# Both products of a squared-ReLU MLP as one level of Strassen, in two phases with the hidden activations in DRAM

## The chip, the core and the metric

The kernel runs on one core of a Trainium2 chip. The metric is the device time of one execution in microseconds (us), taken as the median over the runs. PE is TensorE (matrix products), DVE is VectorE, ACT is ScalarE, POOL is GpSimd and SP is SyncE, which issues most DMAs. Each engine works through its own instructions in order; semaphores order the engines among each other.

## The reference, cut to what matters

The program computes two transformer blocks, one behind the other, on 1024 tokens of width 1024. The part that changes is the MLP of the first block, with the norm behind it and the first norm of the second block. The modulation of the second block does not depend on the tokens, and the kernel computes it beside the MLP.

```python
def sq_relu_mlp(h, up_w, down_w):                  # h 1024x1024, up_w 1024x4096, down_w 4096x1024
    return jnp.square(jax.nn.relu(h @ up_w)) @ down_w

def first_block(...):
    ...
    h = h + sq_relu_mlp(rmsnorm(h, norm_mlp_w), mlp_up_w, mlp_down_w)
    return rmsnorm(h, norm_f_w)

def second_block(x, c, ctx, c_ctx, w_ada, b_ada, ...):
    mod = jax.nn.silu(c) @ w_ada[l] + b_ada[l]             # 1024 x 6144, and the same for c_ctx
    ...
    h = modulate(rmsnorm_2(x, g_mix[l]), sh1, sc1)
    q, k, v, bg, cg, hv = jnp.split(h @ w_in[l], SPLIT_POINTS, axis=-1)
```

## The kernel before

Every product of this kernel is done in three passes: each float32 operand is split into a high part (a copy rounded to fp32r) and a low part (the rest), and `mm3` issues high·high, low·high and high·low into the same PSUM bank (lines L432 to L434). ACT makes the high parts (L419 for weights, L548 for transposed activations), DVE the low parts (L426, L555). A matmul has 128x128 stationary values and 512 moving columns.

The MLP stands in `mlp_block(f)` on PE, ACT and DVE, for eight blocks of 512 hidden features. On PE a block is 192 matmuls of the up product (8 tiles of 128 features by 512 tokens, with 8 slices of the inner dimension and 3 passes each), then 192 of the down product (8 tiles of 128 tokens, 2 halves of 512 columns, 4 slices, 3 passes). Behind each up tile ACT takes the ReLU out of PSUM (L1252), DVE squares it (L1858), ACT makes its high part (L1244) and DVE its low part (L1829): the hidden activations never leave SBUF. Behind each down tile DVE adds the tile to the residual rows `x_tokens` in SBUF (L1872). SP loads the weights of the next half block while this one runs. The blocks 2 to 6 are hardware loops.

Beside the blocks the modulation is summed: POOL loads `ada_w` in 48 pieces of 512 KB, DVE multiplies each with one column per row and adds it to `ada_sums` (L1844 for the first, L1847 for the others, four instructions a piece while both vectors c and c_ctx are summed, then two), and once per block PE sums the partitions in up to four small matmuls (L2590), which ACT copies out (L1263).

Ahead of the MLP the last projection of the attention (`gemm_tokens(B_XO + 1, ...)`) runs over the eight tiles of 128 tokens. Behind each tile come its residual add (L650), the norm (ACT L515 and L518, DVE L526), eight transposes on PE (L541), and high and low parts. Behind the MLP the final norm of block one (ACT L586, DVE L595) and the first norm of block two (L515, L526, and the shift row L530) run row by row beside the last block, and the query projection of block two starts when the first rows are transposed. The projection to keys and values, with 256 columns a matmul, follows it.

Of the kernel before, what the change touches and what calls it, by code (L numbers as in the profile page):

```python
# [29 lines left out]
P = 128  # L30
S = 1024
# [69 lines left out]
def build(nc, x, mem, positions, norm_mix_w, w_in, conv_w, conv_b, conv_ln_w, conv_ln_b, ret_gn_w, w_out,  # L101
# [6 lines left out]
    acc_d = nc.dram_tensor("expert_sums", (S, D), F32, kind="Internal").ap()  # L108

# [189 lines left out]
    with ExitStack() as stack:  # L299
# [41 lines left out]
        T_ML = len(owners)  # L341
        for _ in range(NFB):
            plan(8, "a")
            plan(16, "d")
# [3 lines left out]
        B_I2 = B_ML + 2 * NFB  # L348
        B_W2 = B_I2 + 5
        LAST = {}  # L350
        for b_, n_ in ((B_IN, T_C + 8), (1, T_C + 16), (2, T_QK + 8), (3, T_V + 8), (4, T_G + 8), (B_WO, T_WO + 8),
                       (B_WO + 1, T_WO + 16), (B_KV, T_MK + 4), (B_KV + 1, T_MK + 8), (B_KV + 2, T_MV + 2),
                       (B_KV + 3, T_MV + 4), (B_XQ, T_XQ + 8), (B_XR, T_XR + 8), (B_XO, T_XO + 8),
                       (B_XO + 1, T_XO + 16), (B_ML, T_ML + 8), (B_ML + 1, T_ML + 24), (B_I2 - 1, T_ML + 24 * NFB),
                       (B_I2, T_Q2 + 8), (B_I2 + 1, T_CG + 4), (B_I2 + 2, T_HV + 4), (B_I2 + 3, T_BG + 4),
                       (B_I2 + 4, T_BG + 8), (B_W2, T_W2 + 8), (B_W2 + 1, T_W2 + 16)):
            LAST[b_] = n_ - 1
# [72 lines left out]
        def mm3(o_, lh, ll, rh, rl, start, stop):  # L430
# [3 lines left out]
            return nc.tensor.matmul(o_, ll, rh, start=False, stop=stop)  # L434

# [232 lines left out]
        ada_n, ada_free, ada_acc = sem("ada_products"), sem("ada_piece_used"), sem("ada_acc")  # L668
# [21 lines left out]
        u_sq, u_hi, u_lo = sem("hidden_squared"), sem("hidden_hi_made"), sem("hidden_lo_made")  # L690
# [41 lines left out]
        def _(sp):  # L732
# [20 lines left out]
            def up_piece(f, half):  # L753
                return mlp_up_w[:, bass.ds(f * FB, FB)].rearrange("(k p) n -> p k n", p=P)[:, 4 * half:4 * half + 4, :]

            def down_piece(f, half):
                return mlp_down_w[bass.ds(f * FB + 2 * P * half, 2 * P), :].rearrange("(k p) n -> p k n", p=P)

            def two_rows(half):
                return raw[:, half, :, :].rearrange("p (k a) n -> p k (a n)", a=2)  # L760

            for half in range(2):
                sp_load(B_ML, half, mlp_up_w[:, 0:FB].rearrange("(k p) n -> p k n", p=P)[:, 4 * half:4 * half + 4, :])
            with sp.Fori(0, NFB - 1) as f:
                for half in range(2):
                    sp.wait_ge(w_ready, f * 8 + 4 * B_ML + 2 * (half + 1))
                    sp.dma_start(two_rows(half), down_piece(f, half)).then_inc(w_raw[half], 16)
                for half in range(2):
                    sp.wait_ge(w_ready, f * 8 + 4 * (B_ML + 1) + 2 * (half + 1))
                    sp.dma_start(raw[:, half, :, :], up_piece(f + 1, half)).then_inc(w_raw[half], 16)  # L770
            for half in range(2):
                sp.wait_ge(w_ready, 4 * (B_I2 - 2) + 2 * (half + 1))
                sp.dma_start(two_rows(half), mlp_down_w[(NFB - 1) * FB + 2 * P * half:(NFB - 1) * FB + 2 * P * (half + 1), :]
                             .rearrange("(k p) n -> p k n", p=P)).then_inc(w_raw[half], 16)
            for b in range(B_I2, B_W2 + 2):
                for half in range(2):
                    src, w = w_source(b, half)
                    sp_load(b, half, src, w)
# [46 lines left out]
        def _(pool):  # L825
# [86 lines left out]
            row(GAIN[:, :], norm_mlp_w, gain_in)  # L912
            pool.wait_ge(nm_tp, 2 * N_B2)
            pool.wait_ge(bias_in, 32)

            def mod_store(f, i):

                pool.wait_ge(mod_made, 2 * (f - 1) + (i + 1))
                pool.sem_inc(pool_link, 1)
                pool.dma_start(mod_d[:, bass.ds(1024 * (f - 1) + 512 * i, 512)], MODB[64 * i:64 * i + 2, i, :],  # L920
                               accum_op=ALU.add).then_inc(mod_out[i], 16)

            def ada_loads(f, first=False):

                for i in range(8):
                    if not first:
                        pool.wait_ge(ada_free, 8 * (f - 1) + (i - 1))
                    elif i >= 2:
                        pool.wait_ge(ada_free, i - 1)
                    k = 2 * (i % 4)  # L930
                    pool.dma_start(ADR[:, i % 2, :, :], w_ada_2[0, P * k:P * (k + 2), bass.ds(1024 * (f - 1) + 512 * (i // 4), 512)]
                                   .rearrange("(k p) n -> p k n", p=P)).then_inc(ada_in[i % 2], 16)
                    if i == 1 and not first:
                        mod_store(f - 1, 1)
                mod_store(f, 0)

            ada_loads(1, first=True)
            with pool.Fori(2, NFB - 1) as f:
                ada_loads(f)
            mod_store(NFB - 2, 1)  # L940
            for n in range(2):
                pool.wait_ge(mod_out[n], 16 * (ADA_COLS // 2))
            row(GAIN[:, :], g_mix_2[0], mod_in)
            row(XN[:, 0, :], mod_d[0, D:2 * D], mod_in)
            row(SHIFT[:, :], mod_d[0, 0:D], mod_in)
            row(GF[:, :], norm_f_w, mod_in)

            pool.wait_ge(acc_ready, T_ML + 24 * NFB)
            pool.dma_start(CX[:, 0, :], ctx_2[0, tok(0), :]).then_inc(rows_in, 16)
            pool.dma_start(CX[:, 1, :], ctx_2[0, tok(1), :]).then_inc(rows_in, 16)  # L950
            row(GC[:, :], g_mix_2[0], rows_in)
            row(CSC[:, :], mod_d[1, D:2 * D], rows_in)
            row(SHC[:, :], mod_d[1, 0:D], rows_in)
            for t in range(NT):
                pool.wait_ge(pl_x, t + 1)
                pool.dma_start(xsave_d[tok(t), :], X[:, t, :]).then_inc(x_saved, 16)
            pool.wait_ge(x_saved, 16 * NT)
# [76 lines left out]
        def _(act):  # L1034
# [204 lines left out]
            residual_act(B_XO, T_XO, N_MLP)  # L1239

            def hidden_hi(m, f):
                h, c = m // 4, m % 4
                act.wait_ge(u_sq, f * 8 + m + 1)
                act.activation(UH[:, c, h * 512:(h + 1) * 512], UF[:, m % 2, :], ACT.Copy).then_inc(u_hi, 1)  # L1244

            def mlp_block(f):
                for m in range(8):
                    if m == 7:
                        split_hi(B_ML + 1, off=2 * f)
                    act.wait_ge(acc_ready, f * 24 + T_ML + m + 1)  # L1250
                    act.wait_ge(u_lo, f * 8 + m + 1)
                    act.activation(UF[:, m % 2, :], acc(T_ML + m), ACT.Relu).then_inc(acc_act, 1)  # L1252
                    if m >= 1:
                        hidden_hi(m - 1, f)
                hidden_hi(7, f)

            def mod_copy(f, i, first=False):

                act.wait_ge(ada_acc, 2 * (f - 1) + 2)
                if not first:  # L1260
                    act.wait_ge(mod_out[i], 16 * (f - 1))
                rows = slice(64 * i, 64 * i + 2)
# [1724 lines left out]
```

## Time and profile before

| | |
|---|---|
| median of 3 runs | 2503.62 us (2503.07 to 2506.1) |
| span of the profiled execution, first to last instruction | 2512.2 us |
| PE busy in the span | 97% |
| DVE, ACT, POOL busy in the span | 65%, 42%, 9% |
| TensorE clock granted over the span | 0.985 of full |

All stretches and durations below come from the one profiled execution, whose span is 2512.2 us, 0.34% over the median. Only its span is known, no time around it. A window is given as two times from the start of the span; the MLP of the first block runs from about 697 to 1408 us in it.

### The profile page before, as it was taken

The numbers are of one execution on the slowest core, as the hardware profiler recorded it, in microseconds if no ns is written. First come the engines' busy times: TensorE is split into PE (matmuls) and PEld (weight loads), VectorE is DVE, ScalarE is ACT, GpSimd is POOL, SyncE is SP. The second block draws the span as 40 slices with busy tenths as digits, with TensorE's granted clock in tenths as the row PEclk, the third lists the DMA queues.
The fourth block names the chain that finished last, engine by engine and source line by source line (L and its number), as shares of the span: only waits on it lengthen the run. The fifth ranks groups of instructions, "written<-read, shape, count | busy, mean of one in ns | idle before, by whom it ended". The sixth has DMA issues, their size and how long they took to land.

```text
span 2512.2 us, 31048 instructions
## 1 busy us (share of the span) xinstructions
PE 2442.1 (97%) x12148; PEld 2003.7 (80%) x12148; DVE 1621.1 (65%) x2049; ACT 1056.6 (42%) x1549; POOL 224.7 (9%) x232
## 2 busy tenths in 40 slices
PE   9999899999999999999999999999999999999996
PEld 7788788888888888888888798866786888888884
DVE  7999834324444564444444862477467999999987
ACT  5234523433331222212123422176254777777765
POOL 1000600000000000001010100000113121111101
PEclk9999899999999999999999999999998999999998
DMA  4110221401121232323231311010228999999988
GB/s 154 67 43 34 81 86 43 151 18 42 34 84 57 90 105 84 101 83 117 84 99 69 143 35 51 34 35 18 86 110 306 365 381 398 393 395 394 394 330 304
DMA packets 116317, 370.27 MB, mean 147 GB/s; under 512 B 6309, under 2 KB 15701, under 8 KB 116208
## 3 DMA queue, kind: packets, MB, share of 16 engines
q1 hardware_dynamic: 94832, 293.63, 30.9%
q0 software_dynamic: 21376, 75.12, 9.5%
q8 instruction: 77, 1.26, 0.2%
q14 instruction: 32, 0.26, 0.0%
HBM read 343.50 MB, written 25.26 MB: 147 GB/s over the span
## 4 chain that ended last, share of the span: by engine, by line
PE 86%; DVE 9%; ACT 2%; DMA 2%; issue 1%; SPq 0%; POOLq 0%; DVEq 0%; ACTq 0%
PE banks L432 24%; PE banks L434 24%; PE banks L433 24%; DVE conv_out L1618 3%; PE banks L2769 1%; PE banks L541 1%; PE banks L2567 1%; PE banks L2534 1%; PE banks L2736 1%; DVE w_lo L426 1%; DVE expert_w_lo L2187 1%; PE banks L2702 1%; PE banks L2703 1%; DMA expert_w<-in_w_up 1%; PE banks L2429 1%
## 5 line engine op out<-in xcount | busy, mean ns | idle before, releaser
L2187 DVE TENSOR_TENSOR expert_w_lo<-expert_w,expert_w_hi 128x2048 fp32r<-128x2048 f32 x189 | 426.8, 2285 | 27.3 <-ACT expert_w_hi L1452 26.0
L1452 ACT ACTIVATE expert_w_hi<-expert_w 128x2048 fp32r<-128x2048 f32 x192 | 366.9, 1918 | 151.6 <-PE banks L434 127.3
L432 PE MATMUL banks<-act_hi,w_hi 128*128 128x512 f32 x960 | 375.2, 391 | 0.2 <-DVE act_lo L555 0.2
L434 PE MATMUL banks<-act_hi,w_lo 128*128 128x512 f32 x960 | 373.7, 389 | 0.0
L433 PE MATMUL banks<-act_lo,w_hi 128*128 128x512 f32 x960 | 373.5, 389 | 0.0
L419 ACT ACTIVATE w_hi<-w_raw 128x1024 fp32r<-128x1024 f32 x152 | 159.3, 1060 | 262.7 <-PE banks L434 262.7
L432 PE MATMUL banks<-w_hi,act_hi 128*128 128x512 f32 (+1 forms) x640 | 247.8, 387 | 12.7 <-DVE w_lo L426 10.4
L426 DVE TENSOR_TENSOR w_lo<-w_raw,w_hi 128x1024 fp32r<-128x1024 f32 x152 | 188.3, 1251 | 106.5 <-ACT w_hi L419 100.3
L434 PE MATMUL banks<-w_hi,act_lo 128*128 128x512 f32 (+1 forms) x640 | 244.3, 382 | 0.0
L433 PE MATMUL banks<-w_lo,act_hi 128*128 128x512 f32 (+1 forms) x640 | 244.0, 381 | 0.0
L434 PEld LDWEIGHTS banks<-act_hi,w_lo 128*128 128x128 f32 x960 | 180.2, 188 | 37.7
L432 PEld LDWEIGHTS banks<-act_hi,w_hi 128*128 128x128 f32 x960 | 180.2, 188 | 37.4 <-DVE act_lo L555 0.5
L433 PEld LDWEIGHTS banks<-act_lo,w_hi 128*128 128x128 f32 x960 | 180.2, 188 | 37.0
L432 PE MATMUL banks<-expert_w_hi,expert_rows_T_hi 128*128 128x512 f32 x512 | 201.4, 393 | 3.8 <-DVE expert_w_lo L2187 3.3
L432 PE MATMUL banks<-w_hi,hidden_hi 128*128 128x512 f32 x512 | 200.2, 391 | 0.0
L434 PE MATMUL banks<-expert_w_hi,expert_rows_T_lo 128*128 128x512 f32 x512 | 199.5, 390 | 0.0
L434 PE MATMUL banks<-w_hi,hidden_lo 128*128 128x512 f32 x512 | 199.3, 389 | 0.0
L433 PE MATMUL banks<-w_lo,hidden_hi 128*128 128x512 f32 x512 | 199.3, 389 | 0.0
L433 PE MATMUL banks<-expert_w_lo,expert_rows_T_hi 128*128 128x512 f32 x512 | 199.2, 389 | 0.0
L1872 DVE TENSOR_TENSOR x_tokens<-x_tokens,banks 128x512 f32<-128x512 f32 x128 | 86.9, 685 | 146.6 <-PE banks L434 145.3
L1858 DVE TENSOR_TENSOR hidden_f<-hidden_f 128x512 f32<-128x512 f32 x64 | 44.3, 692 | 180.5 <-ACT hidden_f L1252 180.5
L432 PEld LDWEIGHTS banks<-w_hi,act_hi 128*128 128x128 f32 x640 | 121.6, 190 | 37.4 <-DVE w_lo L426 8.8
(442 smaller groups left out, 4147.7 us busy)
## 6 DMA issues: line engine op xcount, KB each, us to landing
expert_w<-in_w_gate SPq DMA_DIRECT2D x32, 2048.0 KB, 11.5
expert_w<-in_w_up SPq DMA_DIRECT2D x32, 2048.0 KB, 11.6
expert_w<-in_w_down SPq DMA_DIRECT2D x32, 2048.0 KB, 11.1
ada_w<-in_w_ada POOLq DMA_DIRECT2D x48, 512.0 KB, 4.2
w_raw<-in_mlp_up_w SPq DMA_DIRECT2D x16, 1024.0 KB, 5.4
w_raw<-in_mlp_down_w SPq DMA_DIRECT2D x16, 1024.0 KB, 4.9
w_raw<-in_w_in SPq DMA_DIRECT2D x10, 1024.0 KB, 5.3
w_raw<-in_w_in SPq DMA_DIRECT2D x18, 512.0 KB, 6.1
```

The lines of the kernel that those rows point to most:

```text
L419: nc.scalar.activation(WH[:, 2 * j:2 * j + 2, 0:width], raw[:, half, 2 * (j % 2):2 * (j % 2) + 2, 0:width], ACT.Copy).then_inc(w_hi, 1)
L426: nc.vector.tensor_tensor(WL[:, 2 * j:2 * j + 2, 0:width], raw[:, j // 2, 2 * (j % 2):2 * (j % 2) + 2, 0:width], WH[:, 2 * j:2 * j + 2, 0: ...
L432: nc.tensor.matmul(o_, lh, rh, start=start, stop=False)
L433: nc.tensor.matmul(o_, lh, rl, start=False, stop=False)
L434: return nc.tensor.matmul(o_, ll, rh, start=False, stop=stop)
L541: m = nc.tensor.transpose(BK[4 + q % banks][:, c * P:(c + 1) * P], (XN[:, i % 2, :] if src is None else src)[:, k * P:(k + 1) * P], IDN)
L1452: act.activation(EWH[ring][:, 2 * j:2 * j + 2, :], EW[slot][:, 2 * j:2 * j + 2, :], ACT.Copy).then_inc(w_hi, 1)
L1618: dve.scalar_tensor_tensor(out=dst, in0=src, scalar=VT[:, c, j:j + 1], in1=dst, op0=ALU.mult, op1=ALU.add).then_inc(conv_n, 1)
L1858: dve.tensor_tensor(UF[:, m % 2, :], UF[:, m % 2, :], UF[:, m % 2, :], ALU.mult).then_inc(u_sq, 1)
L1872: dve.tensor_tensor(xs, xs, acc(n), ALU.add).then_inc(acc_dve, 1)
L2187: dve.tensor_tensor(EWL[slot][:, c, :], EW[slot][:, c, :], EWH[ring][:, c, :], ALU.subtract).then_inc(w_ready, 1)
L2429: m = pe.matmul(y_bank(t)[:, DV * h:DV * (h + 1)], ST[:, t % 2, h, :], V[:, t, DV * h:DV * (h + 1)], start=(t == 0 and h == 0), stop=(h == ...
```

## The change

The MLP is taken out of `mlp_block` and written as two phases, all unrolled.

**Up phase.** Per block of 512 hidden features the product of weights (1024 x 512) and tokens (1024 x 1024) is cut into 2 by 2 quarters and formed from seven products in place of eight (Winograd's form of Strassen), each 256 features x 512 tokens x 512 inner, that is 24 matmuls. The list `UP` orders the 56 products; below, item n is the n-th of them. The sums of token quarters are formed once, beside the last tiles of the attention projection (`act_sums`, `act_parts`, and on POOL `act_lo_pool`); the sums of weight quarters are formed per block by DVE (`up_sums`), three items ahead of PE. Results are added up partly in PSUM, partly by ACT copies from bank to bank (`copy_p1`) and DVE adds (`c22`, `c12`). The squared hidden values go to DRAM (`hid_d`), and the residual rows are parked there too (`xpark_d`).

**Down phase.** Four chunks of the inner dimension, each of seven Strassen products `M1` to `M7`, each product in two items of 24 matmuls: 56 items. DVE forms the sums of hidden and of weight quarters and the low parts (`down_parts`), ACT the high parts (`down_hi`). ACT also writes a product's running sum back into PSUM ahead of it (`seed`) and reads it out behind it (`evict`).

**Behind them.** POOL combines the seven sums in five adds of 128 x 2048 (`f_z`), DVE in six of 128 x 1024 (`x11`, `x21`, `x22`). Only then do the norms start. For token tiles 3 to 7 POOL adds the shift row of the second norm. PE transposes the first row tile ahead of the last down item.

**The modulation.** DVE's pieces stand behind the items listed in `ADA_PIECES`, and PE's small matmuls (`mou_sums`) ahead of the item behind that (`MOD_AT`).

```diff
@@ the two lists @@
+        UP = [("P1", 0), ("P2", 0), ("P1", 1), ("P5", 0), ("P6", 0), ("P7", 0), ("P4", 0), ("P3", 0)]
+        for b_ in range(1, NFB):
+            UP += [("P5", b_), ("P6", b_), ("P2", b_), ("P7", b_)] + ([("P1", b_ + 1)] if b_ + 1 < NFB else []) + [("P4", b_), ("P3", b_)]
...
+        DOWN = [("M3", ("A11",), ("B12", "B22", ALU.subtract)), ("M5", ("A11", "A12", ALU.add), ("B22",)),
+                ("M4", ("A22",), ("B21", "B11", ALU.subtract)), ("M1", ("A11", "A22", ALU.add), ("B11", "B22", ALU.add)),
+                ("M7", ("A12", "A22", ALU.subtract), ("B21", "B22", ALU.add)), ("M2", ("A21", "A22", ALU.add), ("B11",)),
+                ("M6", ("A21", "A11", ALU.subtract), ("B11", "B12", ALU.add))]
...
+            n_ = (0 if UP[k_][0] == "P1" else 1) if q_ < 16 else (2 if UP[k_][0] in ("P6", "P2") else 1)
+            ADA_PIECES[k_] = range(q_, min(q_ + n_, 48))
...
+        MOD_AT = {k_ + 1: q // 4 for k_, qs in ADA_PIECES.items() for q in qs if q % 4 == 3}
@@ PE @@
-            mlp_block(0, first=True)
...
-            mlp_block(NFB - 1, after=lambda t: norm_transpose(N_B2 + t - 3) if t >= 3 else None)
+            for n in range(NU):
+                kind, b = UP[n]
+                pe.wait_ge(u_lo, n + 1)
+                if n in MOD_AT:
+                    mou_sums(MOD_AT[n])
...
+                        if n == 0 and j == 0 and k == 3:
+                            up_banks_read(6)
+                            begin_banks()
...
+                    if n == 0 and j == 0:
+                        up_transpose(7)
...
+            for n in range(ND - 1):
+                down_sub(n)
+            pe.wait_ge(d_ev, d_ev0 + 2 * (NP - 2))
+            pe.wait_ge(xf, xf0 + 6)
+            norm_transpose(N_B2)
+            down_sub(ND - 1)
+            norm_transpose(N_B2 + 1)
@@ DVE, up phase @@
+            for k in range(NU):
...
+                if done == "P7":
+                    c22(db, 1)
+                if done == "P3":
+                    c12(db, 1)
+                if k + 3 < NU:
+                    up_sums(k + 3)
+                    up_lo(k + 3)
...
+                if kind == "P3":
+                    c12(b, 0)
+                for q in ADA_PIECES.get(k, ()):
+                    ada_piece(q)
@@ ACT, down phase @@
+            for k in range(ND - 4):
+                g = k // 2
+                if k % 2 == 0 and g >= 1:
+                    evict(g - 1, 1)
+                down_hi(k + 3)
+                if k % 2 == 0 and g + 1 in SEED_NO:
+                    seed(g + 1)
+                if k % 2 == 1 and g < NP - 3:
+                    evict(g, 0)
@@ POOL @@
+            for t in range(4, NT):
+                act_lo_pool(t)
...
+            pool.tensor_tensor(DACC["M6"], DACC["M1"], DACC["M3"], ALU.add).then_inc(f_z, 1)
+            pool.wait_ge(f_z, f_z0 + 4)
+            pool.wait_ge(d_ev, d_ev0 + 2 * m7 + 2)
+            pool.tensor_tensor(DACC["M6"], DACC["M6"], DACC["M2"], ALU.subtract).then_inc(f_z, 1)
```

Three places show how the instructions stand.

DVE in the up phase, around items 5 to 8, after the change (`up_w_lo` are low parts of weight operands three items ahead, `hidden_stage_dve` the adds and squares of finished hidden tiles, `ada_sums` the modulation):

```order
L2358 SCALAR_TENSOR_TENSOR ada_sums<-ada_w,silu_c,ada_sums 128x512 x4
L2273 TENSOR_TENSOR up_w_lo<-up_w_123,up_w_hi 128x1024
L2380 TENSOR_TENSOR hidden_stage_dve<-up_sum_u_136,banks 128x512
L2364 SCALAR_TENSOR_TENSOR hidden_stage_dve<-hidden_stage_dve 128x512
L2358 SCALAR_TENSOR_TENSOR ada_sums<-ada_w,silu_c,ada_sums 128x512 x4
L2380 TENSOR_TENSOR hidden_stage_dve<-up_sum_u_136,banks 128x512
L2364 SCALAR_TENSOR_TENSOR hidden_stage_dve<-hidden_stage_dve 128x512
L2294 TENSOR_TENSOR up_w_sums<-up_w_odd,up_w_121 128x1024
L2273 TENSOR_TENSOR up_w_lo<-up_w_sums,up_w_hi 128x1024
```

The second `ada_sums` row is the last of the first four pieces: it stands last in DVE's step beside item 7, and PE's small matmuls ahead of item 8 wait for it. Before the change the pieces stood between adds to the residual:

```order
L1872 TENSOR_TENSOR x_tokens<-x_tokens,banks 128x512 x2
L1847 SCALAR_TENSOR_TENSOR ada_sums<-ada_w,silu_c,ada_sums 128x512 x4
L1872 TENSOR_TENSOR x_tokens<-x_tokens,banks 128x512 x2
L1847 SCALAR_TENSOR_TENSOR ada_sums<-ada_w,silu_c,ada_sums 128x512 x4
L1872 TENSOR_TENSOR x_tokens<-x_tokens,banks 128x512 x6
```

There the small matmuls came behind the sixth of the eight token tiles, and a piece was only followed by residual adds and low parts of later weights.

ACT in the down phase, one product of two items after the change (L1614 high parts, L1624 reads a product out of PSUM, L1645 writes the running sum of a later one into PSUM):

```order
L1624 ACTIVATE x_tokens<-banks 128x2x512 x2
L1614 ACTIVATE down_a_hi<-down_a_sums 128x1024
L1614 ACTIVATE t_hi<-t_plain 128x1024
L1645 ACTIVATE banks<-x_tokens 128x1024 x2
L1614 ACTIVATE down_a_hi<-down_a_sums 128x1024
L1614 ACTIVATE act_hi<-act_hi_plain 128x2x512
L1624 ACTIVATE act_lo_plain<-banks 128x2x512 x2
```

None of these stood there before: the residual was added by DVE (L1872).

DVE at the end of the down phase, after the change (the first row is the low part of the last item's operand; L634 and L565 are the rows of the two norms, L2443 are adds of `x21`):

```order
L2405 TENSOR_TENSOR t_lo<-t_plain,t_hi 128x1024
L2483 SCALAR_TENSOR_TENSOR second_gain_row<-x_normed,second_gain_row 128x1024
L633 RECIPROCAL rms_scale<-root_mean_square 128x1
L634 SCALAR_TENSOR_TENSOR x_tokens<-x_tokens,rms_scale,gain_row_final 128x1024
L633 RECIPROCAL rms_scale<-root_mean_square 128x1
L634 SCALAR_TENSOR_TENSOR x_tokens<-x_tokens,rms_scale,gain_row_final 128x1024
L563 RECIPROCAL rms_scale<-root_mean_square 128x1
L565 SCALAR_TENSOR_TENSOR x_normed<-x_tokens,rms_scale,second_gain_row 128x1024
L569 TENSOR_TENSOR x_normed<-x_normed,second_shift_row 128x1024
L633 RECIPROCAL rms_scale<-root_mean_square 128x1
L634 SCALAR_TENSOR_TENSOR x_tokens<-x_tokens,rms_scale,gain_row_final 128x1024
L2443 TENSOR_TENSOR x_tokens<-x_tokens,banks 128x2x512
```

Behind these come the row tile 1 (L563, L565, L569) and the second L2443. The first transposes of PE wait until that second L2443 is done, and the last down item stands behind the transposes. Before, the norms ran row by row beside the last block's matmuls.

## Rows read from the trace of the kernel before

**Rows 1.** The page, part 1: busy time, share of the span, instructions

```profile
PE 2442.1 (97%) x12148; PEld 2003.7 (80%) x12148; DVE 1621.1 (65%) x2049; ACT 1056.6 (42%) x1549; POOL 224.7 (9%) x232
```

**Rows 2.** Windows: busy time by engine, granted clock, DMA share, GB/s

```profile
697.00:1408.00 711.00, 711.00 (x3155) 582.12 (x3154) 358.02 (x488) 170.97 (x258) 47.58 (x64) 1.00 0.26 86
```

**Rows 3.** The chain that ended last, in order of time: start us, us

```profile
1129.38 0.96 PE banks L2590 x4
...
1217.60 0.96 PE banks L2590 x4
```

**Rows 4.** Timeline of PE behind the MLP; brackets: idle before, releaser

```profile
1413.15 0.39 PE L434 MATMUL banks<-w_hi,act_lo 128*128 128x512 f32 x1
1419.80 0.80 PE L432 MATMUL banks<-w_hi,act_hi 128*128 128x512 f32 x1 [6.26 <-DVE w_lo L426]
...
1468.13 0.39 PE L432 MATMUL banks<-w_hi,act_hi 128*128 128x256 f32 x1 [0.26 <-DVE w_lo L426]
```

**Rows 5.** Windows behind that wait, and behind the later one of rows 6

```profile
1420.00:1424.00 4.00, 4.00 (x11) 3.17 (x12) 3.71 (x4) 0.00 (x0) 0.53 (x1) 0.59 1.03 408
...
1638.00:1642.00 4.00, 3.94 (x23) 3.48 (x21) 3.35 (x8) 4.00 (x12) 0.00 (x0) 0.57 0.01 2
```

**Rows 6.** Timeline of PE in the second block's attention

```profile
1637.28 0.38 PE L2702 MATMUL banks<-w_k_hi_T,act_hi 128*128 128x256 f32 x1 [3.29 <-ACT w_probs L1359]
```

**Rows 7.** Groups of DVE instructions by line and form: busy us, mean ns

```profile
L426 DVE TENSOR_TENSOR w_lo<-w_raw,w_hi 128x1024 fp32r<-128x1024 f32 x152 | 188.3, 1251 | 106.5 <-ACT w_hi L419 100.3
L1872 DVE TENSOR_TENSOR x_tokens<-x_tokens,banks 128x512 f32<-128x512 f32 x128 | 86.9, 685 | 146.6 <-PE banks L434 145.3 <-DVE ada_sums L1847 1.2
L526 DVE SCALAR_TENSOR_TENSOR x_normed<-x_tokens,rms_scale,gain_row 128x1024 f32<-128x1024 f32 x39 | 50.1, 1285 | 1.4
```

**Rows 8.** Timeline of DVE: instructions back to back, in single rows of several

```profile
695.82 4.62 DVE L426 TENSOR_TENSOR w_lo<-w_raw,w_hi 128x1024 fp32r<-128x1024 f32 x4
...
835.16 1.37 DVE L1872 TENSOR_TENSOR x_tokens<-x_tokens,banks 128x512 f32<-128x512 f32 x2 [0.45 <-PE banks L434]
...
894.20 2.73 DVE L1847 SCALAR_TENSOR_TENSOR ada_sums<-ada_w,silu_c,ada_sums 128x512 f32<-128x512 f32 x4
```

**Rows 9.** Timeline of ACT at the end of the MLP

```profile
1406.40 3.89 ACT L419 ACTIVATE w_hi<-w_raw 128x1024 fp32r<-128x1024 f32 x4
...
1413.40 1.06 ACT L586 ACTIVATE squares_row<-x_tokens 128x1024 f32<-128x1024 f32 x1 [2.15 <-DVE x_tokens L1872]
1414.36 0.19 ACT L586 ACTIVATION_READ_ACCUMULATOR squares_row<-x_tokens 128x1 f32 x1
1414.58 0.29 ACT L588 ACTIVATE root_mean_square<-sum_squares,eps_col 128x1 f32<-128x1 f32 x1
```

**Rows 10.** Groups of ACT instructions that read PSUM

```profile
L1252 ACT ACTIVATE hidden_f<-banks 128x512 f32<-128x512 f32 x64 | 38.2, 596 | 242.1 <-PE banks L434 241.9 <-DVEq L1894 0.2
...
L1462 ACT ACTIVATE expert_silu<-banks 128x1024 f32<-128x1024 f32 x16 | 16.1, 1006 | 2.2 <-PE banks L434 2.2
```

**Rows 11.** Timeline of POOL beside the conv and the retention

```profile
274.52 2.52 POOL L863 TENSOR_TENSOR conv_out<-conv_out,conv_ln_rstd 128x512 f32<-128x512 f32 x2
276.97 0.75 POOL L883 TENSOR_TENSOR ret_q_decayed<-ret_qk_T,ret_consts 128x256 f32<-128x256 f32 x1
277.66 1.28 POOL L872 TENSOR_TENSOR ret_gate<-ret_gate,ret_gn_row 128x512 f32<-128x512 f32 x1
...
282.29 3.47 POOL L863 TENSOR_TENSOR conv_out<-conv_out,conv_ln_rstd 128x512 f32<-128x512 f32 x2
```

**Rows 12.** Timeline of DVE in the same stretch

```profile
275.15 4.87 DVE L426 TENSOR_TENSOR w_lo<-w_raw,w_hi 128x1024 fp32r<-128x1024 f32 x1
...
283.12 1.51 DVE L426 TENSOR_TENSOR w_lo<-w_raw,w_hi 128x1024 fp32r<-128x1024 f32 x1
```

**Rows 13.** Groups of POOL: the largest elementwise instruction of the kernel before

```profile
L998 POOL TENSOR_TENSOR expert_w_lo<-expert_w,expert_w_hi 128x2048 fp32r<-128x2048 f32 x3 | 13.5, 4548 | 0.0
```

**Rows 14.** The page, DMA issues: KB each, median us to landing

```profile
w_raw<-in_mlp_up_w SPq DMA_DIRECT2D x16, 1024.0 KB, 5.4
```

More of the change, by code:

```diff
@@ new lines, in build, with sub_done @@
+        NCH = 4
+        NP = 7 * NCH
+        ND = 2 * NP
+        SUM_NO, SEED_NO = {}, {}
+        for n_ in range(ND):
+            for side_ in (1, 2):
+                if len(DOWN[n_ // 2 % 7][side_]) == 3:
+                    SUM_NO[n_, side_] = 4 * NFB + len(SUM_NO) + 1
+        for g_ in range(NP):
+            if g_ >= 7 or g_ not in (0, 3, 5):
+                SEED_NO[g_] = 2 * len(SEED_NO)
+        def sub_done(n):
+            return 2 * NU + 3 * (n // 2) + (1 if n % 2 == 0 else 3)
@@ L764, in _, with up_w @@
[L764 to L774, printed above, removed]
+            def up_w(b, kh, fh):
+                c = 512 * b + 256 * fh
+                return mlp_up_w[512 * kh:512 * (kh + 1), c:c + 256].rearrange("(k p) n -> p k n", p=P)
@@ L923, in ada_loads @@
[L923 to L940, printed above, removed]
+                pool.dma_start(mod_d[:, 512 * cb:512 * (cb + 1)], MODB[64 * (cb % 2):64 * (cb % 2) + 2, cb % 2, :],
+                               accum_op=ALU.add).then_inc(mod_out[cb % 2], 16)
+            for q in range(4 * ADA_COLS):
+                if q >= 2:
+                    pool.wait_ge(ada_n, ada_ops(q - 1))
+                kk = 2 * (q % 4)
+                pool.dma_start(ADR[:, q % 2, :, :], w_ada_2[0, P * kk:P * (kk + 2), 512 * (q // 4):512 * (q // 4 + 1)]
+                               .rearrange("(k p) n -> p k n", p=P)).then_inc(ada_in[q % 2], 16)
+                if q >= 4 and q % 4 == 2:
+                    mod_store(q // 4 - 1)
@@ new lines, in second_lo @@
+            def second_lo(t):
+                norm_lo(N_B2 + t, a_hi(t), a_lo(t))
+            dve.wait_ge(mod_in, 64)
+            dve.scalar_tensor_tensor(out=GAIN2[:, :], in0=XN[:, 0, :], scalar=1.0, in1=GAIN2[:, :], op0=ALU.add,
+                                     op1=ALU.mult).then_inc(gain_made, 1)
+            dve.wait_ge(gain_made, 1)
+            first_rows(0)
+            first_rows(1)
+            second_rows(0)
+            first_rows(2)
+            x21(0)
+            second_rows(1)
```

948 lines of the change are left out of this document (739 added, 209 removed).

## The prediction

> **What bounds the kernel now.** I began with the page: PE is busy 97% of the span, DVE 65%, ACT and POOL far less [rows 1]. A share over the span says nothing of one stage, so next came the window of the MLP. In its 711 us PE is busy for all 711 at a granted clock of 1.00, DVE for 358, ACT for 171, POOL for 48 [rows 2]: the stage is bound by the number of matmuls and by nothing else. The chain in time order gives their price. The modulation matmuls of two successive blocks begin 88.22 us apart, and they take 0.96 [rows 3], so 384 matmuls last 87.26 us, 0.2272 each, and 24 of them, an item of the new program, 5.45.
>
> Behind the MLP the timeline of PE shows the one real stall: 6.26 us for the low part of a query weight that stands behind the norm rows in DVE's queue, later another 0.26 [rows 4]. The window behind the first shows what such idleness costs beyond itself: clock 0.59 of full, and 11 matmuls in 4 us where 17.6 fit [rows 5], 1.5 us lost. A wait of 3.29 us elsewhere [rows 6] is followed by 0.57 as well [rows 5]. Stalls of some 3 us therefore have a tail; 0.26 had none in view.
>
> **What is removed.** The products go from 8 x 384 matmuls to 112 items of 24, that is 3072 to 2688: 384 fewer, **−87.3 us**. Two matmuls that open PSUM banks add **+0.5**. The 12 modulation sums stay. The end of the MLP is rewritten, so its old stalls go: 6.26 + 1.5 + 0.26 = **−8.0**. All else must be paid out of these 94.8 us, and is paid by DVE, ACT and POOL.
>
> **Start of the up phase.** Unit prices first. A 128x1024 DVE instruction with two SBUF inputs takes 1.16 back to back (4.62 for four), a 128x512 one 0.69, a modulation piece of four 2.73 [rows 8]. On ACT a 128x1024 copy takes 0.97 (3.89 for four) [rows 9], a 128x512 one out of PSUM 0.60 [rows 10]. For each of the token tiles 4 to 7 DVE now has six differences (4.1), the residual add (0.7) and the norm row (1.3, [rows 7]), 6.1 us in the time of a tile, 5.45 plus its transposes. So it has no reserve, and ahead of the last tile three low parts (3.5) are put in as well. PE then waits for the norm of tile 6, for the differences of tile 6 ahead of the bank openers in item 0, and for the norm of tile 7 behind half of item 0. I estimate 1.4, 1.4, 4.0 and 2.0 plus 1.2 at the lower clock, **+10**; bounds 0 (all in reserve of the three items of lead) and 16 (the whole 3.5 + 6.1 + 6.1). POOL's twelve small differences there, 1.28 each by [rows 11], can hold DVE up: +2, bounds 0 and 4. Taken **+12**.
>
> **Up phase.** A block of seven items takes PE 38.1 us. DVE's work for one: three sums, one further sum and seven low parts (11 x 1.16 = 12.8), eight instructions on finished hidden tiles (5.5), six or seven modulation pieces (16.4 to 19.1): 34.7 to 37.4. That fits barely, and each sum must go to ACT and come back before its low part. The operands have three items of lead, which covers this. The modulation has none: the fourth piece of a column block stands last in DVE's step beside item k, and PE's sums stand ahead of item k+1. Beside item 7, ACT first reads a tile, copies two banks, squares two (5 x 0.60) and makes the high part (0.97); DVE's low part (1.16), add and square (1.4) and the piece (2.73) follow: 9.2 us from the item's start against 5.45, a wait of 3.8. Item 22 repeats it; items 12 and 17 give about 2.8. The eight later sums have pieces of half the length, and I put them at 1 each with the waits of P5 for the adds of the block before: 13.2 + 8 = 21. Two of the waits are as long as the 3.29 with a tail of 1.5 each: **+24**. Bounds 0 (if ACT's share is done ahead of time) and 35 (every step late by as much as the worst, 2.8 for all twelve).
>
> **Down phase.** Per item DVE has three or four instructions of 1.16, at most 4.6 of 5.45; ACT per product four high parts, two seeds and two reads of 128x1024: 4 x 0.97 + 4 x 1.0 (PSUM reads 1.006 [rows 10]; a write into PSUM of this size has no row, between 0.97 and twice that) = 7.9 of 10.9. Loads on SP's queue are 512 KB, a 1024 KB one lands in 5.4 us [rows 14], against a lead of 16. So **0**. What hides ACT is its 3.0 us of slack per product; gone, each further microsecond costs 28.
>
> **End.** The norms used to run row by row beside the last block's matmuls. Now nothing can start before the seven sums are combined. The transposes ahead of the last item wait for the second x21 add. Behind its last operand DVE has a gain row (1.2), three final-norm rows and two second-norm rows (five of 1.29, and two shifts of 1.16), and two adds of 1.16: 12.3, with the reciprocals between them about 13, and some 3.3 of ACT statistics (1.06 + 0.19 + 0.29 each [rows 9]) that nothing covers. DVE's own step beside item 52 (four instructions and an add, 5.9) stands ahead, so the chain ends 22.2 us after item 52's start; PE is through items 52 to 54 after 16.3: a wait of 5.9, plus a tail of 1.5. The context rows now come last and hold up their transposes by 1 to 3, and the first weight for keys and values waits for them (5): **+14**, bounds 8 and 20. POOL's five adds of 128x2048, 4.55 each [rows 13], fall into the same stretch. [rows 12] show what that can do: a low part of 1.25 mean [rows 7] took 4.87 while POOL ran three instruction groups back to back at their normal pace, and another took 1.51 while POOL's pair took 3.47 instead of 2.52 [rows 11]. So either may lose. On the chain DVE can lose 17 (two POOL adds and most of two more) or 0; I take **+9**, the middle, since the two rows disagree on the loser. Five shift rows on POOL, 2.3 each as half of 4.55, mostly beside the query matmuls: **+2.5**, bounds 0 and 12.
>
> The Trainium skill, "SBUF — State Buffer", section "Who interferes with whom", says that a DVE instruction with two SBUF inputs contends with a GpSimd instruction that reads SBUF, and under an exclusive lock. The 4.87 agrees with a lock, the 1.51 only partly; by the rule alone the nine would be up to seventeen.
>
> **Sum:** −87.3 + 0.5 − 8.0 + 12 + 24 + 14 + 9 + 2.5 = −33.3 us, so the profiled execution of 2512.2 would become 2479. That span is 8.6 us above the median of the runs shown; the same difference taken from 2503.6 gives **2470 us**.
>
> **The rivals.**
>
> *B, the vector engines keep pace* (0.18). If ACT's copies run ahead and POOL yields, the up phase costs 8, the start 10, the end 14: gain 94.8 − 32 = 63, about 2441. For it: DVE's total fits into 38.1 per block. Against: its order in the queue, which no average changes.
>
> *C, the port and the queues cost their upper part* (0.20). DVE blocked for 17 at the end, 6 for shift rows, start 16, up phase 30, end 14: 83, gain 12, about 2491; at still higher prices within 5 us of no change. For it: [rows 12]. Against: POOL lost in one of the two.
>
> *D, ACT's queue becomes the bound of the down phase: slower* (0.09). ACT's high part waits for a DVE sum, and the seed of the next product stands behind it. With 3.0 us of slack and 28 products, the gain of 33 is gone when a product takes ACT 3.0 + 1.2 = 4.2 us more than its 7.9, and at 5 more the time is 2470 + 28 x 2 = 2526. For it: the sums start only when the buffer of an item earlier is free, so four trips from DVE to ACT and back fall into each product. Against: each trip has three items to do so.
>
> That the change does not do what it says is excluded here: the program holds 2688 of these matmuls.
>
> **How the numbers follow.** The forecast has 0.50, with its own range of 2456 to 2484; B 0.18, around 2441; C 0.20, of which 0.04 within 5 us of 2503.6; D 0.09; the remaining 0.03 near no change. Faster and slower count from 0.2%, or 5 us, about what this kernel's measurement can tell from no change: faster 0.50 + 0.18 + 0.16 = 0.84, same 0.07, slower 0.09. The range of 2436 to 2497 leaves out a little of B, D and the part of C near no change, 0.2 together.
>
> **What would show it.** PE busy should fall by some 87 us in the stretch from 690 to 1470, and waits of PE should appear: of `mou_sums` for `ada_sums`, 2 to 4 us each at items 8, 12, 17 and 22; of the bank openers for act_lo; of the first transposes for `x_normed` at the end, 6 to 15 us; and none in the down phase. DVE rows of 128x1024 well over 1.3 us beside POOL's 128x2048 adds show the port; if they stay at 1.2 while POOL's exceed 4.6, POOL yields and the 9 goes. Waits of the down items for `seed` or high parts would show D. The prediction is wrong if the up phase stalls in most items, if the clock stays low beyond the tails, or if PE waits for its own instructions now that no loop repeats them, for which I have no row.

## The result, and the profile after

The changed kernel takes 2516.56 us (median of 8), the kernel before 2504.07 beside it. The ratio is 1.005 with a 95% interval of 1.0032 to 1.0067: slower by half a per cent, some 12.5 us, where 2470 had been forecast. The profiled execution has a span of 2528.0 us, 15.8 more than that of before; it is the slowest of its eight. Up to the first transposes of the MLP's norm the two traces are level (659.54 us before, 659.72 after). At the first scores of the second block's attention the changed kernel is 12.5 us behind (1625.1 and 1637.6); the other 3.3 lie behind that, where the program is the same.

The page of the changed kernel, part 1:

```profile
PE 2396.9 (95%) x11766; PEld 1948.2 (77%) x11766; DVE 1798.4 (71%) x2092; ACT 1259.3 (50%) x1759; POOL 282.9 (11%) x254
```

Against [rows 1], PE has 382 instructions fewer and is busy 45 us less: the matmuls did go, but those that are left take longer. PE's idle time, span less busy time, rose from 70 to 131 us, so 45 saved and 61 lost make the 16 of the span. The waits of PE in the stretch from the last attention projection to the first keys and values (us in total, times, longest):

```profile
PE banks L3213 <- issue: 25.3, 9, 4.2
PE banks L580 <- DVE x_tokens L2443: 15.5, 1, 15.5
PE banks L471 <- ACT banks L1645: 5.2, 2, 4.7
PE banks L3195 <- DVE x_normed L565: 4.4, 3, 1.5
PE banks L580 <- DVE ctx_rows L569: 3.5, 1, 3.5
PE banks L465 <- DVE w_lo L459: 3.0, 1, 3.0
PE banks L3245 <- ACT t_hi L1530: 2.4, 1, 2.4
```

L3213 are the modulation matmuls, L580 the transposes (first the row tile 0 of block two, then the context rows), L1645 is a `seed`, L3245 the bank openers. "issue" means that the view names no releaser; the timelines name it. PE and then DVE around item 8:

```profile
760.88 0.39 PE L473 MATMUL banks<-act_hi,up_w_lo 128*128 128x512 f32 x1
764.97 3.42 PE L3213 MATMUL banks<-ada_sums,consts_sb 128*2 128x512 f32 x4 [3.69 <-issue]
768.32 0.50 PE L471 MATMUL banks<-act_hi,up_w_hi 128*128 128x512 f32 x1
```

```profile
759.67 1.22 DVE L2273 TENSOR_TENSOR up_w_lo<-up_w,up_w_hi 128x1024 fp32r<-128x1024 f32 x1 [2.43 <-ACT up_w_hi L1510]
760.81 0.68 DVE L2380 TENSOR_TENSOR hidden_stage_dve<-up_sum_u,banks 128x512 f32<-128x512 f32 x1
761.52 0.69 DVE L2364 SCALAR_TENSOR_TENSOR hidden_stage_dve<-hidden_stage_dve 128x512 f32<-128x512 f32 x1
762.13 2.73 DVE L2358 SCALAR_TENSOR_TENSOR ada_sums<-ada_w,silu_c,ada_sums 128x512 f32<-128x512 f32 x4
```

DVE's piece ends at 764.86 and PE goes on at 764.97: this is the wait that was forecast, of the size that was forecast (3.8). What was not forecast stands in the same row: the modulation matmuls themselves, four rows of the trace (each such matmul is recorded as two), take 3.4 us, where four took 0.96 before [rows 3]. The groups of these matmuls before and after, busy us and mean ns, then idle time ahead of them:

```profile
L2590 PE MATMUL banks<-ada_sums,consts_sb 128*2 128x512 f32 x32 | 7.9, 592 | 0.0
```

```profile
L3213 PE MATMUL banks<-ada_sums,consts_sb 128*2 128x512 f32 x32 | 23.0, 837 | 25.3 <-issue 25.3
```

The window over the stretch with all modulation sums, granted clock behind the engines' busy times:

```profile
764.00:1030.00 266.00, 241.45 (x954) 178.63 (x955) 174.32 (x217) 90.07 (x129) 40.90 (x54) 0.94 0.56 172
```

In [rows 2] that clock was 1.00. At the end of the down phase DVE's and POOL's timelines read:

```profile
1351.13 1.23 DVE L2397 TENSOR_TENSOR down_a_sums<-act_lo_plain,w_raw 128x1024 f32<-128x1024 f32 x1 [0.66 <-PE banks L473]
1353.54 4.38 DVE L2405 TENSOR_TENSOR down_a_lo<-down_a_sums,down_a_hi 128x1024 fp32r<-128x1024 f32 x1 [1.19 <-ACT down_a_hi L1614]
1357.84 5.63 DVE L2405 TENSOR_TENSOR act_lo<-act_hi_plain,act_hi 128x1024 fp32r<-128x1024 f32 x1
1363.39 5.61 DVE L2397 TENSOR_TENSOR down_a_sums<-act_lo_plain,w_raw 128x1024 f32<-128x1024 f32 x1
...
1386.48 4.40 DVE L634 SCALAR_TENSOR_TENSOR x_tokens<-x_tokens,rms_scale,gain_row_final 128x1024 f32<-128x1024 f32 x1
...
1399.16 5.40 DVE L569 TENSOR_TENSOR x_normed<-x_normed,second_shift_row 128x1024 f32<-128x1024 f32 x1
```

```profile
1351.15 5.68 POOL L1180 TENSOR_TENSOR x_tokens<-x_tokens 128x2048 f32<-128x2048 f32 x1 [0.29 <-ACT banks L1645]
1356.91 5.48 POOL L1182 TENSOR_TENSOR x_tokens<-x_tokens,act_hi_plain 128x2048 f32<-128x2048 f32 x1
1362.35 5.57 POOL L1184 TENSOR_TENSOR x_tokens<-x_tokens,act_lo_plain 128x2048 f32<-128x2048 f32 x1
1384.86 4.93 POOL L1186 TENSOR_TENSOR x_tokens<-act_lo_plain,act_hi_plain 128x2048 f32<-128x2048 f32 x1 [16.94 <-ACT banks L1645]
1398.49 4.99 POOL L1189 TENSOR_TENSOR x_tokens<-x_tokens,x_top_right 128x2048 f32<-128x2048 f32 x1 [8.70 <-ACT x_top_right L1624]
```

Lay the two side by side: each of the five long DVE rows ends 1.1 us behind the end of one POOL row, about the time that the DVE instruction takes alone. Once a POOL add has begun, a DVE instruction with two SBUF inputs gets through nothing until it ends. The order of the starts matters: the DVE row of 1351.13 began 0.02 us ahead of POOL's first add and took its normal 1.23. Five rows lose about 19 us to it (4.38 + 5.63 + 5.61 + 4.40 + 5.40, less five of 1.2 to 1.3).

### The profile page after: what moved, and what is told of

It reads as the page before. It is cut to its first block, busy times and chain, and to the rows that moved or that the text cites. A ratio compares the mean times of both kernels' runs of the same rounds, so it can differ in the third digit from the quotient of the medians.

```text
span 2528.0 us, 30286 instructions
## 1 busy us (share of the span) xinstructions
PE 2396.9 (95%) x11766; PEld 1948.2 (77%) x11766; DVE 1798.4 (71%) x2092; ACT 1259.3 (50%) x1759; POOL 282.9 (11%) x254
## 4 chain that ended last, share of the span: by engine, by line
PE 76%; DVE 14%; issue 4%; ACT 3%; DMA 1%; POOL 0%; POOLq 0%; SPq 0%; ACTq 0%; DVEq 0%
PE banks L465 15%; PE banks L467 15%; PE banks L466 15%; PE banks L471 6%; PE banks L472 6%; PE banks L473 6%; DVE conv_out L2064 3%; PE banks L3430 1%; PE banks L3179 1%; PE banks L3146 1%; DVE w_lo L459 1%; PE banks L3397 1%; DVE expert_w_lo L2799 1%; PE banks L3213 1%; PE banks L580 1%
## 5 line engine op out<-in xcount | busy, mean ns | idle before, releaser
L465 PE MATMUL banks<-w_hi,act_hi 128*128 128x512 f32 (+1 forms) x640 | 249.3, 389 | 10.5 <-DVE w_lo L459 7.0
L465 PE MATMUL banks<-expert_w_hi,expert_rows_T_hi 128*128 128x512 f32 x512 | 202.2, 395 | 4.0 <-DVE expert_w_lo L2799 3.6
L465 PE MATMUL banks<-act_hi,w_hi 128*128 128x512 f32 x448 | 175.9, 393 | 0.2 <-DVE act_lo L594 0.2
L467 PE MATMUL banks<-act_hi,w_lo 128*128 128x512 f32 x448 | 174.6, 390 | 0.0
L466 PE MATMUL banks<-act_lo,w_hi 128*128 128x512 f32 x448 | 174.5, 389 | 0.0
L2064 DVE SCALAR_TENSOR_TENSOR conv_out<-conv_in,vectors_T,conv_out 128x1024 f32<-128x1024 f32 (+1 forms) x138 | 148.7, 1142 | 3.4 <-ACT conv_out L1312 2.9
L465 PEld LDWEIGHTS banks<-w_hi,act_hi 128*128 128x128 f32 x640 | 122.5, 191 | 35.4 <-issue 7.1
L467 PEld LDWEIGHTS banks<-w_hi,act_lo 128*128 128x128 f32 x640 | 122.3, 191 | 23.5
L466 PEld LDWEIGHTS banks<-w_lo,act_hi 128*128 128x128 f32 x640 | 122.6, 192 | 22.3 <-issue 0.2
L465 PEld LDWEIGHTS banks<-expert_w_hi,expert_rows_T_hi 128*128 128x128 f32 x512 | 96.4, 188 | 24.6 <-DVE expert_w_lo L2799 4.5
L467 PEld LDWEIGHTS banks<-expert_w_hi,expert_rows_T_lo 128*128 128x128 f32 x512 | 96.6, 189 | 20.4
L466 PEld LDWEIGHTS banks<-expert_w_lo,expert_rows_T_hi 128*128 128x128 f32 x512 | 96.7, 189 | 19.4
L471 PE MATMUL banks<-act_hi,up_w_hi 128*128 128x512 f32 x256 | 104.9, 410 | 5.3 <-DVE hidden_stage_dve L2380 2.3
L472 PE MATMUL banks<-act_lo,up_w_hi 128*128 128x512 f32 x256 | 102.6, 401 | 0.0
## 6 DMA issues: line engine op xcount, KB each, us to landing
expert_w<-in_w_up SPq DMA_DIRECT2D x32, 2048.0 KB, 11.4
```

Of the source, the lines that this page charges most:

```text
L465: nc.tensor.matmul(o_, lh, rh, start=start, stop=False)
L466: nc.tensor.matmul(o_, lh, rl, start=False, stop=False)
L471: nc.tensor.matmul(o_, lh, rh, start=start, stop=False, skip_group_check=True)
L472: nc.tensor.matmul(o_, lh, rl, start=False, stop=False, skip_group_check=True)
L2064: dve.scalar_tensor_tensor(out=dst, in0=src, scalar=VT[:, c, j:j + 1], in1=dst, op0=ALU.mult, op1=ALU.add).then_inc(conv_n, 1)
```

## The experiments

All times are ratios to the kernel before, run on the same chip; the changed kernel has 1.005. A difference of 0.001 is 2.5 us. The intervals reach 0.0015 to 0.0031 to either side, so a difference between two kernels below is known to some 6 or 7 us, with e1 to 9. Gains of a few us are read from the traces, and the times only fail to contradict them.

**e1: the modulation matmuls one item later.** DVE's pieces stay where they are.

```diff
-        MOD_AT = {k_ + 1: q // 4 for k_, qs in ADA_PIECES.items() for q in qs if q % 4 == 3}
+        MOD_AT = {k_ + 2: q // 4 for k_, qs in ADA_PIECES.items() for q in qs if q % 4 == 3}
```

> PE's modulation matmuls stand one item later, nothing else moves. Theory (the pieces have no lead, the operands have three items of it): the nine waits before them (25.3 us in the changed kernel) go, with the lower clock that follows each; the matmuls themselves fall from 23.0 us to about 15, at 0.95 a pair. Time falls by 33 to 42, to 2475 to 2484. Rival (DVE is the bound of the up phase, the waits only stand where they stand): the waits reappear in front of matmuls that want up_w_lo or hidden_stage_dve, and the time stays within 10 of 2516.

Ratio 0.9912 (0.9881 to 0.9943): 35 us less than the changed kernel, and faster than the kernel before. The group of the modulation matmuls, and a window over about the same stretch of the program as above (its end lies some 8 us further on):

```profile
L3213 PE MATMUL banks<-ada_sums,consts_sb 128*2 128x512 f32 x32 | 15.7, 591 | 2.3 <-issue 2.3
```

```profile
750.00:990.00 240.00, 233.94 (x981) 178.30 (x981) 176.45 (x221) 89.34 (x128) 41.02 (x54) 1.00 0.63 193
```

The profiled execution of e1 was already 12.9 us ahead at the first transposes of the MLP's norm (646.82), where the program is unchanged, so the spans can't be compared. The same two matmuls in each kernel can, one ahead of the first modulation sum and one behind the last, first in the changed kernel, then in e1:

```profile
755.67 0.39 PE L471 MATMUL banks<-act_hi,up_w_hi 128*128 128x512 f32 x1
...
1078.20 0.39 PE L471 MATMUL banks<-act_hi,up_w_hi 128*128 128x512 f32 x1
```

```profile
741.10 0.39 PE L471 MATMUL banks<-act_hi,up_w_hi 128*128 128x512 f32 x1
...
1029.64 0.39 PE L471 MATMUL banks<-act_hi,up_w_hi 128*128 128x512 f32 x1
```

322.5 us became 288.5: the 34.0 us of this stretch are the gain. In it the waits for the sums fall by 23.0 and the modulation matmuls by 7.3; some 6 come from the matmuls behind, with the clock back at 1.00. The waits do not come back elsewhere: those for `hidden_stage_dve` rise only from 3.1 to 5.3 us in all, which takes 2 off again. DVE was not the bound of the up phase. One item of lead was missing.

**e11: the output rows of the modulation matmuls, in the kernel before.** There the two column blocks of a pair wrote rows 0 and 64 of two banks.

```diff
-                        m = pe.matmul(BK[6 + i][64 * i:64 * i + 2, :], ...
+                        m = pe.matmul(BK[6 + i][0:2, :], ...
```

> The kernel before, with one thing changed: the modulation matmuls of the second column block write output rows 0 and 1, as the first does, and no longer rows 64 and 65; ACT and POOL read them there. Theory (two of these matmuls run side by side when their output rows are 64 apart, and one after the other when not): the group of 32 rows rises from 7.9 us busy to about 15.5, four of them from 0.96 to 1.8; time slower by 5 to 9, 2509 to 2513. Rival (they were quick because they alternated between two banks, which they still do): 7.9 us stays, and the time too.

Ratio 1.0021 (1.0001 to 1.004). The group, and four of them in the chain in time order:

```profile
L2590 PE MATMUL banks<-ada_sums,consts_sb 128*2 128x512 f32 x32 | 14.7, 592 | 0.0
```

```profile
1131.23 1.81 PE banks L2590 x4
```

The time is 5 us (0 to 10) over the kernel before, as forecast. 0.96 became 1.81, although the two banks still alternate. So the pairs had run side by side because their output rows lay 64 apart; the change, which sums one column block at a time, put them one behind the other. Each single row lasts 592 ns in the kernel before and in e11, and 591 in e1: a mean per instruction does not show it, the busy time of the group does.

**e2: POOL's five adds left out.** The output lacks these sums.

```diff
-            pool.tensor_tensor(DACC["M7"], DACC["M4"], DACC["M5"], ALU.subtract).then_inc(f_z, 1)
...
+            pool.sem_inc(f_z, 3)
...
+            pool.sem_inc(f_z, 2)
```

> POOL's five adds of 128x2048 are left out, so the output lacks these sums; everything that waited for them still waits for what they waited for. Theory (POOL's adds hold DVE up through the shared port): DVE's rows of 4.4 to 5.6 us go back to 1.2, PE's wait of 4.75 for a seed goes, the wait of 15.5 ahead of the first transposes falls to about 8; time falls by 12 to 17, to 2500 to 2505. Rival (the chain of norms alone sets that wait, the long rows only look long because DVE waits for something else): under 4 us, and the long rows stay.

Ratio 0.9973 (0.9956 to 0.999): 19 us less, where 12 to 17 had been expected. DVE's row that had taken 5.63, and the last shift row:

```profile
1348.22 1.22 DVE L2400 TENSOR_TENSOR act_lo<-act_hi_plain,act_hi 128x1024 fp32r<-128x1024 f32 x1
...
1374.47 1.23 DVE L569 TENSOR_TENSOR x_normed<-x_normed,second_shift_row 128x1024 f32<-128x1024 f32 x1
```

The seed's wait of 4.7 is gone, and the wait ahead of the transposes is 5.1 in place of 15.5, less than the 8 expected here and close to the 5.9 that the prediction had for the chain without POOL.

**e3: the five adds on DVE.**

```diff
+                if k == ND - 7:
+                    f_z1()
+                if k == ND - 6:
+                    f_z2()
+                if k == ND - 5:
+                    f_z3()
```

(`f_z1` to `f_z5` hold POOL's instructions and waits; the last two stand behind the second x21 and ahead of the first x22.)

> The same five adds on DVE in place of POOL: three in its steps beside items 49 to 51, two behind the second x21 add. Theory (port): DVE works 11.6 us more and loses none of the 20 that it lost to POOL; the seed's wait goes or shrinks under 2, the wait ahead of the transposes is 8 to 12; time falls by 4 to 10, to 2506 to 2512. Rival (DVE's queue is the chain at the end, more work on it costs as much): no change within 3, or slower.

Ratio 1.0021 (1.0006 to 1.0036): 7 us less than the changed kernel. DVE does each add in 2.28 us, 11.4 in all, and no row beside them is long; the wait ahead of the transposes is 9.6. Time, adds and wait came as expected. The adds are cheaper there than the 19 us that they cost on POOL.

**e4: all shift rows on DVE.**

```diff
-        SHIFT_POOL = 3
+        SHIFT_POOL = NT
```

> All eight shift rows of the second norm on DVE; in the changed kernel tiles 3 to 7 had them on POOL. Theory (port): DVE works 5 x 1.2 us more and gets back some 2.2 on each of five rows that took 3.45 beside POOL, so the waits of 3.5 for the context rows and 3.0 for the first low part of the key weights shrink by 3 to 5 together; time falls by 2 to 6, to 2511 to 2515. Rival (DVE is what everything waits for there, so its own five rows cost the 6 us that POOL had hidden): slower by 2 to 6.

Ratio 1.0019 (1.0004 to 1.0034): 8 us less, where 2 to 6 had been expected; the difference is within the noise. In the changed kernel four rows of the final norm (the expectation says five) started with one of POOL's shift rows and took 3.45:

```profile
1427.02 3.45 DVE L634 SCALAR_TENSOR_TENSOR x_tokens<-x_tokens,rms_scale,gain_row_final 128x1024 f32<-128x1024 f32 x1
```

```profile
1426.99 2.38 POOL L1202 TENSOR_TENSOR x_normed<-x_normed,second_shift_row 128x1024 f32<-128x1024 f32 x1 [2.17 <-DVE x_normed L2476]
```

3.45 is 2.38 and 1.28 less a little. With e4 each takes 1.28, the wait for the context rows falls from 3.5 to 1.5, and one of 1.2 for `act_lo` goes. DVE rows with one input in PSUM were not held up: `rotary_tmp_first<-banks,consts_sb` took its usual 0.41 at 1452.83 and 1453.49, beside POOL's fifth shift row.

**e5: two of three weight operands split behind the last token tile's work.**

```diff
-                        for n in range(3):
-                            up_lo(n)
+                        up_lo(0)
...
+            up_lo(1)
+            up_lo(2)
```

(and the high parts on ACT likewise)

> At the start of the up phase only the first of three weight operands is split ahead of the last token tile's work, the other two behind it, on ACT and on DVE. Theory (three low parts stand in the way of the differences that the bank openers want): the waits of 2.41 ahead of the openers and 1.31 ahead of the last transposes go, with some of the lower clock behind them; time falls by 3 to 6, to 2511 to 2514. Rival (the same waits only move to the matmuls of the next two items): no change within 2.

Ratio 1.0047 (1.0031 to 1.0063): no change. The openers wait 1.6 in place of 2.4, but the third item then waits longer for its bank:

```profile
715.48 0.47 PE L471 MATMUL banks<-act_hi,up_w_hi 128*128 128x512 f32 x1 [3.23 <-ACT hidden_stage_act L1573]
```

In the changed kernel it was 1.89 there. All the start's waits together are 11.0, against 9.8. The rival holds by the trace (the time alone could still hide a gain of 3 to 6): with this order the waits only stand elsewhere.

**e7: the last down item ahead of the first transposes.**

```diff
-            for n in range(ND - 1):
+            for n in range(ND):
                 down_sub(n)
...
             norm_transpose(N_B2)
-            down_sub(ND - 1)
```

> PE does the last down item ahead of the first transposes of the second block, all else as in the changed kernel. Theory (the order on PE leaves a ready item of 5.4 us standing behind a wait for DVE): the wait of 15.5 ahead of the transposes shrinks by 5.4 to about 10, and the two adds of x22 can start earlier; time falls by 5 to 9, to 2508 to 2512. Rival (DVE's later rows set the start of the queries anyway): the wait moves behind the transposes, no change within 3.

Ratio 1.004 (1.0022 to 1.0058), not told apart from the changed kernel, where 5 to 9 us had been expected. The first wait shrinks to 10.2, and a new one stands behind it, of the first query matmul; the view names no releaser, and DVE's first add of x22 ended 0.1 us ahead of it. Together they are 15.3, as long as the one wait before:

```profile
1397.30 3.58 PE L580 MATMUL banks<-consts_sb,x_normed 128*128 128x128 f32 x16 [10.25 <-DVE x_tokens L2443]
1405.94 0.77 PE L465 MATMUL banks<-w_hi,act_hi 128*128 128x512 f32 x1 [5.06 <-issue]
```

**e6, e8, e9, e10: together.** e6 is e1 with e3; e8 adds e4 and e7; e9 is e1, e3 and e4; e10 is e9 with both x21 adds, and ACT's reads of that product, ahead of the second norm's rows.

> The modulation matmuls one item later and POOL's five adds on DVE, both together. Theory (two separate places, 300 us apart): the gains add up, 34 + 5 = 39, so 2475 to 2480. Rival (what is won in the up phase is lost again in front of the norms, since those wait for DVE and ACT): not under 2483.

> Four edits together: modulation matmuls one item later, the five adds and all shift rows on DVE, the last down item ahead of the transposes. Theory: 34 + 5 + 4 + 6 = 49, so 2464 to 2471, faster than the kernel before by 33 to 40. Rival (the end is one chain on DVE, and only one of the three edits there can count): 2474 to 2478.

> Modulation matmuls one item later, the five adds and all shift rows on DVE; the last down item stays behind the first transposes, as in the changed kernel. Theory now (the end is one chain on DVE, and moving the last item on PE only moved the wait): the same as the four edits together within 3, 2472 to 2478. Rival (the last item's place does count once the port is free): slower than the four edits by 4 to 6, 2479 to 2481.

> The same three edits, and at the end DVE does both x21 adds and ACT both reads of that product ahead of the second norm's rows, so PE's first transposes wait for less. If the wait ahead of the transposes (9.6 with the adds on DVE) is the price: it falls to about 5, and the time by 4 to 5 against the three edits. If DVE's whole chain to the later rows is the price: the wait moves behind to the query matmuls and the time stays within 2.5.

| | ratio | interval | median us |
|---|---|---|---|
| e6 | 0.9884 | 0.9864 to 0.9903 | 2478.97 |
| e8 | 0.9874 | 0.9854 to 0.9894 | 2475.09 |
| e9 | 0.9869 | 0.9846 to 0.9892 | 2472.42 |
| e10 | 0.9864 | 0.9842 to 0.9886 | 2475.72 |

e6 is the sum of its two parts (35 and 7). e8, e9 and e10 are one time within their intervals, and e6 overlaps with them. e8 had been expected at 2464 to 2471 us and e10 4 to 5 us under e9; neither came, and the rivals named there did. PE's two waits at the end, first in e9, then e8, then e10:

```profile
PE banks L580 <- DVE x_tokens L2431: 9.6, 1, 9.6
PE banks L465 <- issue: 4.0, 1, 4.0
```

```profile
PE banks L465 <- DVE x_tokens L2438: 9.7, 1, 9.7
PE banks L580 <- issue: 4.1, 1, 4.1
```

```profile
PE banks L465 <- issue: 8.4, 1, 8.4
PE banks L580 <- DVE x_normed L569: 5.2, 1, 5.2
```

L580 are the transposes, L465 the first query matmul, L2431 the adds of x21 and L2438 those of x22. The two waits sum to 13.6, 13.8 and 13.6: a single chain that ends with DVE's adds of x22 fits all three, and neither PE's order nor the place of x21 moves its end. e9, three small edits, is faster than the kernel before by 1.3% (1.1 to 1.5), some 33 us.

## Why the prediction was wrong

**The gain was there.** PE ran 382 matmuls fewer, and the stages without waits held their pace: behind 1030 us the matmuls ran 0.23 us apart, with waits of 0.5 and less until the 53rd item of the down phase. "Down phase: 0" was right up to that item, and D, ACT's queue as the bound, did not come: the wait of 4.7 for a `seed` at the 53rd is 0.5 in e2, so it belongs to POOL's adds.

**The step that failed first is "The 12 modulation sums stay".** Their count stayed, their price did not: 7.9 us busy in the kernel before (the group of L2590, 32 rows), 23.0 after. Half of the rise is the lost overlap (e11: 14.7; e1: 15.7 at full clock), half the lower clock in which a wait leaves PE. I had priced the waits at 21 with those of P5; they were 25.3, and 3.1 for `hidden_stage_dve`. I had taken two tails of 1.5; behind seven of the nine waits the sums ran slower than at full clock (1.4 to 1.9 us for two rows against 1.02 in e1, 3.2 to 3.4 for four against 1.88), and the clock was 0.94 over 266 us. e1 shows waits, slow sums and tails together as 35 us (34.0 in the trace) that one item of lead takes away. Even then 7.8 us of the overlap stay lost. Both together, 43, lie over the upper bound of 35 too; that bound was worked out with 2.8 for each of twelve steps, though the worst step stood at 3.8.

**The second is the port at +9.** I took the middle between 0 and 17, since two rows of before disagreed on who loses. The runs say: in all five places DVE started second and lost, for what was left of POOL's instruction. e2 puts the five adds at 19 us, at the upper bound or over it, and e4 the shift rows at 8 where 2.5 stood (at 4 by e9 beside e6, both within the noise). The rule of the Trainium skill, "SBUF — State Buffer", section "Who interferes with whom", that two-input DVE instructions and GpSimd reads exclude each other, was the better guide than the mean of two rows; in the rows above a blocked DVE instruction ends one own duration after POOL's, as an exclusive lock gives. POOL pays too: each of its five adds began while a DVE row with two SBUF inputs was still under way, by 0.5 to 1.2 us, and took 4.9 to 5.7; less that overlap it is 4.4 to 4.5 each, close to the 4.55 of [rows 13].

**The others.** The norms' chain at the end was sized well (5.9 forecast, 5.1 in e2), as were the waits for the key weights and the context rows (6 to 8 together forecast, 3.0 and 3.5 measured). The start was forecast at 12; its waits sum to 9.8 (1.54, 1.53, 1.13, 2.41, 1.31, 1.89), and the granted clock was 0.76 from 703 to 731 us. e5 shows that its order does not win it.

**The sum.** From −33 to +12.5 is 46 us. The modulation makes about 19 of it (35 in e1 and 7.8 of overlap, against the 24 taken), the adds 10, the shift rows 1 to 6. The last ten to fifteen are not assigned by a run. The lower clock at the start can be part of them: 0.76 over 28 us is at most 6.7 us of matmul time by my estimate, where 1.2 stood. Single waits for `hidden_stage_dve` (3.1) can be another.

Rival C was the nearest in kind, with the port in full and waits in the up phase, and too low in price by 25 us, for want of the overlap and of the tails. D's 2526 us lies nearer in number, but its mechanism did not come.

## What to carry to other kernels

When work is moved, price again what "stays": an instruction's count and duration can be the same and its overlap gone, so compare the busy time of the group of instructions, not the mean of one. A result that one in-order engine makes last in a step and another wants first in the next has no lead at all, however idle both are on average; one step of distance was worth 35 us here. An add that is free on POOL is not free while DVE works on two SBUF operands: look where the two would run at the same time, and do it on DVE if DVE has the time (2.3 us an add here).

## What the runs showed of the hardware that was not expected

Two matmuls of 128x2 stationary values whose output rows lie 64 apart ran side by side: four rows of the trace in 0.96 us, against 1.81 with the same output rows (e11), each row 592 ns in both. The Trainium skill, "TensorEngine Tiling (Array Packing)", section "Key Properties", states that different tiles of the array can execute matmuls in parallel; e11's times agree, though the kernel names no tiles, and no run shows that these two matmuls are such tiles.

At the lower of TensorE's two clock levels (1.2 and 2.4 GHz; the granted clock was 0.50 of full from 921 to 924 us) two rows of the modulation matmuls took 1.87 us, against 1.02 in e1, and the matmuls behind them started 0.43 apart in place of 0.23. PE had waited 3.14 us before that:

```profile
918.85 1.87 PE L3213 MATMUL banks<-ada_sums,consts_sb 128*2 128x512 f32 x2 [3.14 <-issue]
920.65 0.80 PE L471 MATMUL banks<-act_hi,up_w_hi 128*128 128x512 f32 x1
...
921.67 0.63 PE L473 MATMUL banks<-act_hi,up_w_lo 128*128 128x512 f32 x1
922.10 0.63 PE L471 MATMUL banks<-act_hi,up_w_hi 128*128 128x512 f32 x1
```

Taking 23 us of such waits away gave back 34 in the same stretch (e1).

This wait, of 3.14, has another cause beside the order: DVE's piece waited 2.5 us for its weights. The buffer of `ada_w` holds two pieces, so POOL's queue can fetch them no further ahead.

```profile
917.21 1.54 DVE L2358 SCALAR_TENSOR_TENSOR ada_sums<-ada_w,silu_c,ada_sums 128x512 f32<-128x512 f32 x2 [2.52 <-DMA ada_w<-in_w_ada]
```
